# A two-block transformer kernel: the softmax of block 2's first layer normalised on GpSimd ahead of the transposes

## What is computed

```python
q = apply_rope(rms_norm(heads(aq, N_Q_HEADS), q_norm), cos, sin)
k = apply_rope(rms_norm(heads(ak, N_KV_HEADS), k_norm), cos, sin)
y_a = global_gqa(q, k, v, k_c, v_c)        # 256 sequence rows attend to sequence and context
y_ca = context_attention(q_c, k_c, v_c)    # 256 context rows attend to the context only
```

## Time and profile before

| | |
|---|---|
| median of 3 runs | 1485.29 us (1481.9 to 1487.43) |
| profiled execution, its own time | 1483.27 us |
| its span, first to last instruction | 1481.5 us |
| TensorE matmul busy | 1419.3 us, 96% of the span |
| TensorE weight load busy | 1150.1 us, 78% |
| one low part of the weights on VectorE (L1902), mean of 344 | 1.213 us |
| VectorE, ScalarE, GpSimd busy | 917.6, 773.5, 152.7 us |
| mean granted clock of TensorE | 0.987 of full |

### The profile page before, as it was taken

One profiled execution on the slowest core, in us unless ns is written; L12 is line 12 of the kernel. 1 busy time (PEld: TensorE's weight loads), 2 busy tenths in 40 slices (PEclk: granted clock), 3 DMA queues, 4 the chain that ended last, 5 costly groups with the idle time before them and its releaser, 6 DMA issues.

```text
span 1481.5 us, 21298 instructions
## 1 busy us (share of the span) xinstructions
PE 1419.3 (96%) x8232; PEld 1150.1 (78%) x8232; DVE 917.6 (62%) x1618; ACT 773.5 (52%) x1281; POOL 152.7 (10%) x188
## 2 busy tenths in 40 slices
PE   7999989999999999998999999999999789999998
PEld 6887767799887787776789978787777348777776
DVE  4555668666544554566856666577553775669665
ACT  5445776455444444687445545334456322544873
POOL 6040000000000000000000000002000660132220
PEclk9999999999999999999999999999999899999999
DMA  9784326697555755332689654463223001255100
GB/s 280 253 189 121 121 90 246 180 272 212 185 185 171 281 174 169 96 130 89 238 243 250 194 181 164 167 170 86 58 80 92 25 1 57 73 164 142 58 30 29
DMA packets 183555, 220.29 MB, mean 149 GB/s; under 512 B 6667, under 2 KB 103477, under 8 KB 183456
## 3 DMA queue, kind: packets, MB, share of 16 engines
q1 hardware_dynamic: 179376, 211.65, 45.4%
q0 software_dynamic: 3040, 7.28, 2.6%
q10 hardware_dynamic: 1040, 0.00, 0.0%
HBM read 215.90 MB, written 3.01 MB: 148 GB/s over the span
## 4 chain that ended last, share of the span: by engine, by line
PE 41%; DVE 8%; ACT 3%; issue 2%; POOL 1%; DVEq 0%; ACTq 0%
PE bank L634 10%; PE bank L636 10%; PE bank L635 10%; PE bank L1150 2%; PE bank L1113 1%; DVE w_low L1902 1%; PE bank L1126 1%; PE bank L651 1%; DVE arena L2322 1%; PE bank L1289 1%; ACT w_high L1430 1%; PE bank L721 1%; DVE arena L2419 1%; PE bank L1309 0%; PE bank L1297 0%
## 5 line engine op out<-in xcount | busy, mean ns | idle before, releaser
L1902 DVE TENSOR_TENSOR w_low<-raw,w_high 128x1024 fp32r<-128x1024 f32 x344 | 413.4, 1213 | 296.1 <-ACT w_high L1430 292.0
L1430 ACT ACTIVATE w_high<-raw 128x1024 fp32r<-128x1024 f32 x352 | 364.8, 1046 | 327.2 <-PE bank L636 257.9
L634 PE MATMUL bank<-w_high,acts_r 128*128 128x512 f32 (+1 forms) x848 | 342.5, 404 | 19.3 <-DVE arena L2153 10.7
L636 PE MATMUL bank<-w_high,acts_r 128*128 128x512 f32 (+1 forms) x848 | 332.7, 392 | 0.0
L635 PE MATMUL bank<-w_low,acts_r 128*128 128x512 f32 (+1 forms) x848 | 332.5, 392 | 0.0
L634 PE MATMUL bank<-acts_r,w_high 128*128 128x256 f32 (+1 forms) x736 | 229.8, 312 | 1.3 <-DVE arena L2381 1.3
L636 PE MATMUL bank<-acts_r,w_low 128*128 128x256 f32 (+1 forms) x736 | 226.5, 308 | 0.0
L635 PE MATMUL bank<-acts_r,w_high 128*128 128x256 f32 (+1 forms) x736 | 225.4, 306 | 0.0
L634 PEld LDWEIGHTS bank<-w_high,acts_r 128*128 128x128 f32 x848 | 161.0, 190 | 67.1 <-DVE arena L2153 13.3
L636 PEld LDWEIGHTS bank<-w_high,acts_r 128*128 128x128 f32 x848 | 161.3, 190 | 37.2
L635 PEld LDWEIGHTS bank<-w_low,acts_r 128*128 128x128 f32 x848 | 161.6, 191 | 32.9 <-issue 0.2
(11 more groups left out here) (331 smaller groups left out, 1713.1 us busy)
## 6 DMA issues: line engine op xcount, KB each, us to landing
raw<-in_w_in SPq DMA_DIRECT2D x69, 1024.0 KB, 5.1
raw<-in_w_up SPq DMA_DIRECT2D x64, 512.0 KB, 6.9
raw<-in_w_down SPq DMA_DIRECT2D x32, 1024.0 KB, 4.9
raw<-in_w_ada SPq DMA_DIRECT2D x24, 1024.0 KB, 7.7
raw<-in_w_in SPq DMA_DIRECT2D x34, 512.0 KB, 5.1
raw<-in_w_o SPq DMA_DIRECT2D x8, 1024.0 KB, 8.0
raw<-in_w_out SPq DMA_DIRECT2D x8, 1024.0 KB, 5.0
raw<-in_w_out_c SPq DMA_DIRECT2D x4, 768.0 KB, 4.9
```

The lines of the kernel that those rows point to most:

```text
L634: mm(o, lh, rh, start=start, stop=False)
L636: return mm(o, ll, rh, start=False, stop=stop)
L1430: run(A_(high, src, ACT.Copy), (high_ready, n + 1))
L1902: run(V.tensor_tensor(low, src, high.bitcast(F32), ALU.subtract), split_done(n))
```

## The change

In layer 0 of block 2 GpSimd multiplies each unit's exponentials, in place, by the inverse of their sum, as soon as VectorE has inverted it; the transposes wait for that (`probs_scaled`). The product that spreads the inverse sums, ScalarE's copy of it and VectorE's product with it are dropped; VectorE copies the PSUM result instead. GpSimd's other work of this stretch is put between the pairs: the four folds behind pair 5, the five DMAs behind pair 12.

```diff
@@ second
-                    pe.wait_ge(*probs_at(2 + l, u))
+                    pe.wait_ge(*(probs_at(3, u) if l else (probs_scaled, u + 1)))
@@ values
-                    pe.wait_ge(*pair_inverted.at(2 + l, i))
+                    if l:
+                        pe.wait_ge(*pair_inverted.at(3, i))
...
-                    for side in range(2):
+                    for side in range(2 if l else 0):
                         inverse = stat[:, (u + side) % 4, 3, 1:2].to_broadcast([P, DH])
                         ins = mm(o[side * DH:(side + 1) * DH, P:2 * P], inverse, ident[:, :], start=True, stop=True)
@@ attention2 of ScalarE
-                    if i >= 2:
+                    if l and i >= 2:
                         spread_sums(i - 2)
...
-                spread_sums(PAIRS - 1)
+                if l:
+                    spread_sums(PAIRS - 1)
@@ take_values
-                    dve.wait_ge(*sum_spread.at(2 + l, i))
-                    run(V.tensor_tensor(dst, o[:, 0:P], spread[:, :], ALU.mult), emptied("o", 2 + l, i))
+                    if l == 0:
+                        dve.wait_ge(*filled("o", 2, i))
+                        run(V.tensor_copy(dst, o[:, 0:P]), emptied("o", 2, i))
+                        return
+                    dve.wait_ge(*sum_spread.at(3, i))
+                    run(V.tensor_tensor(dst, o[:, 0:P], spread[:, :], ALU.mult), emptied("o", 3, i))
@@ GpSimd's list
-            for c in range(4):
-                pool.wait_ge(*emptied("in2f", 0, c))
-                z = uc[:, c, :].rearrange("p (s n) -> p s n", s=2)
...
-            pool.wait_ge(*filled("s", 2, 22))
-            pool.wait_ge(*filled("s", 2, 23))
-            pool.dma_start(decay.rearrange("p t n -> p (t n)"), C["decay"]).then_inc(decay_loaded, 16)
...
+            for i in range(PAIRS):
+                pool.wait_ge(*pair_inverted.at(2, i))
+                for u in (2 * i, 2 * i + 1):
+                    row = S4[:, u % 4, 0:SEQ if units_of_block2(0)[u][2] >= TILES else N4]
+                    G.tensor_scalar(row, row, stat[:, u % 4, 3, 1:2], None, ALU.mult).then_inc(probs_scaled, 1)
+                if i == 5:
+                    for c in range(4):
+                        pool.wait_ge(*emptied("in2f", 0, c))
+                        z = uc[:, c, :].rearrange("p (s n) -> p s n", s=2)
...
+                if i == 12:
+                    pool.wait_ge(*filled("s", 2, 22))
+                    pool.wait_ge(*filled("s", 2, 23))
+                    pool.dma_start(decay.rearrange("p t n -> p (t n)"), C["decay"]).then_inc(decay_loaded, 16)
...
```

More of the change, by code:

```diff
@@ L461, in two_blocks @@
         pair_inverted = Signal(sem("pair_inverted"), soft_pairs + [(l, i) for l in (2, 3) for i in range(len(units_of_block2(l - 2)) // 2)])
-        sum_spread = Signal(sem("sum_spread"), soft_pairs + [(l, i) for l in (2, 3) for i in range(len(units_of_block2(l - 2)) // 2)])
+        sum_spread = Signal(sem("sum_spread"), soft_pairs + [(3, i) for i in range(len(units_of_block2(1)) // 2)])
+        probs_scaled = sem("probs_scaled")
         stick_summed = Signal(sem("stick_summed"), sticks)
@@ L1149, in values @@
                                 v = nv[:, b, h * DH:(h + 1) * DH]
-                            mm(o[side * DH:(side + 1) * DH, 0:P], v, PT2[:, side, n * P:(n + 1) * P], start=n == 0, stop=n == len(blocks) - 1)
-                    for side in range(2):
+                            ins = mm(o[side * DH:(side + 1) * DH, 0:P], v, PT2[:, side, n * P:(n + 1) * P],
+                                     start=n == 0, stop=n == len(blocks) - 1)
+                    for side in range(2 if l else 0):
                         inverse = stat[:, (u + side) % 4, 3, 1:2].to_broadcast([P, DH])
@@ L2728, in _ @@
                 pool.dma_start(dst, src).then_inc(hidden_loaded, 16)
-            for c in range(4):
-                pool.wait_ge(*emptied("in2f", 0, c))
-                z = uc[:, c, :].rearrange("p (s n) -> p s n", s=2)
[L2732 to L2737, removed]
-            pool.wait_ge(*filled("s", 2, 22))
-            pool.wait_ge(*filled("s", 2, 23))
-            pool.dma_start(decay.rearrange("p t n -> p (t n)"), C["decay"]).then_inc(decay_loaded, 16)
-            for n in range(4):
-                pool.dma_start(w3[n], A["hy_w3_2"][0][:, n * HY:(n + 1) * HY]).then_inc(w3_loaded, 16)
+            for i in range(PAIRS):
[7 more added lines that the diff above has]
+                        z = uc[:, c, :].rearrange("p (s n) -> p s n", s=2)
+                        left, right, right_back = z[:, :, 0:P], z[:, :, P:SEQ], z[:, :, SEQ - 1:P - 1:-1]
+                        run(G.tensor_tensor(left, left, right_back, ALU.subtract))
+                        run.settle()
+                        run(G.tensor_tensor(right, right, right, ALU.add))
+                        run.settle()
+                        run(G.tensor_tensor(right_back, right_back, left, ALU.add), (z_folded, c + 1))
+                if i == 12:
+                    pool.wait_ge(*filled("s", 2, 22))
+                    pool.wait_ge(*filled("s", 2, 23))
+                    pool.dma_start(decay.rearrange("p t n -> p (t n)"), C["decay"]).then_inc(decay_loaded, 16)
+                    for n in range(4):
+                        pool.dma_start(w3[n], A["hy_w3_2"][0][:, n * HY:(n + 1) * HY]).then_inc(w3_loaded, 16)
             for i in range(PAIRS):
```

## The result

| | before | changed |
|---|---|---|
| median of 4 runs each | 1483.6 us (1481.8 to 1487.4) | 1499.0 us (1496.9 to 1501.0) |
| ratio to before, 95% interval | | 1.0095 (1.0077 to 1.0114) |
| profiled execution | 1483.27 us | 1496.92 us |
| its span | 1481.5 us | 1495.1 us |

The change makes the kernel 0.95% slower, 15.4 us in the medians. The profiled execution of the changed kernel is the fastest of its four, so the profiles explain 13.65 us and not the 1.8 us more of the medians. The forecast was 1491, 0.4%, with a range from 1484 to 1500. Every line number of the attention has moved by a few in the changed file: scores are L1114, transposes L1127, values L1152, the reciprocal L2446, the multiply L2741, low parts L1906.

A forecast was written before the change was run, and what follows sets the result against it. TensorE's own list was taken to set the attention's pace: -4.2 us gained, +8.6 waits and +1.7 clock make +6.1 us, which against the median of 1485.3 gave 1491 us, range 1484 to 1500.

The forecast's parts named there:

- rival 3: GpSimd's multiplies are slow, growing with columns: at 1.6 us waits of 18 us, +17, 1502 us in all; chance 0.10.
- What a multiply costs: GpSimd's multiply by a scalar from SBUF: taken as 1.0 us for 512 columns and 0.7 for 256.
- rival 1: GpSimd's multiplies are short, 0.6 to 0.8 us; only pairs 0 and 6 wait notably; +1.6, 1487 us; chance 0.20.
- Wide after narrow: Transposes of pairs 4 and 8: 9.69 us from scores against TensorE's 8.95, wait 0.75 us each, 1.5.
- Wide after wide: Transposes of pairs 5 and 9: a loop of 8.85 us against TensorE's 8.14, wait 0.7 us each, 1.4.
- Pairs 12 and 13: Wide pairs with one product where the convolution's four stood: 8.6 us, under 8.95, so no wait.
- Pair 1: Like pair 9, but with four more late-head transposes (0.44 us) in its round: wait 0.3 us.
- Narrow pairs: Transposes of narrow pairs fit without a wait: 7.83 us against TensorE's 7.92.
- Pair 0: First pair's transposes wait 2.1 us for the multiplies, its reciprocal counted 0.4 us earlier because the folds leave this place.
- Pair 6: Its multiplies queue on GpSimd behind pair 5's multiplies and four folds; TensorE waits 3.3 us, the costliest pair.
- The gain: Dropped inverse-sum products free TensorE 0.28 us a pair (0.24 to 0.32), 15 counted: -4.2 us.
- The clock: A low-clock stretch after TensorE's waits in pairs 0 and 6: one drop counted (none to two), +1.7 us.

The follow-up runs named there:

- experiment 2: Changed kernel with its four folds spread, one each behind pairs 2, 3, 6 and 7, not all behind pair 5: 1492.7 us, ratio to before 1.0062.
- experiment 3: Changed kernel with VectorE's reciprocal of pair 0 alone moved ahead of its round's low parts and convolution products: 1495.8 us, ratio to before 1.008.
- Experiment 1: Changed kernel without GpSimd's multiplies and without the wait for them, output left undivided: 1479.4 us, ratio to before 0.9974.
- experiment 5: Changed kernel with GpSimd multiplying only the first half of each row, 256 of 512 columns or 128 of 256: 1489.8 us, ratio to before 1.0034.
- experiment 6: Changed kernel with the multiplies on VectorE right behind the reciprocal, GpSimd keeping folds and DMAs: 1482.1 us, ratio to before 0.9986.
- experiment 4: Changed kernel with every reciprocal of this layer ahead of its round's low part and features, folds spread behind pairs 2, 3, 6, 7: 1481.1 us.
- experiment 7: Changed kernel with every reciprocal of this layer ahead of its round's low part and features, folds still behind pair 5: 1481.9 us.
- experiment 8: Changed kernel with the multiplies on VectorE and every reciprocal ahead of the low part: 1481.4 us, ratio to before 0.9979.

## Why the forecast came out as it did

The direction, the place and the mechanism of the waits were right; the size was short, by 7.6 us in the profiled executions (13.65 against 6.1). Of these, 5.9 are waits, 0.9 the gain and 0.7 the clock. That the median still lies within the range, 1 us from its end, is partly luck. The range was laid on a median before of 1485.3, which came out as 1483.6. The measured 15.4 us on top of that would be 1500.7. The sum's own bounds ended at +12 us, and rival 3, whose multiplies these were, was left out of the range with a chance of 0.10. By the forecast's steps:

- **What a multiply costs** is the step that failed. It was taken as 1.0 and 0.7 us, from one multiply of 128 columns and the price of a column in a memset, and is 1.56 and 0.92: a column costs 2.5 ns, twice the memset's 1.21. The row of 0.542 us for 128 columns was a good guide (0.603 here); the slope laid on it was not. The bound named for two tensors, 1.276 us for 512 columns, was no bound: one tensor and a scalar from SBUF take longer. Rival 3, with 1.6 us, described this run: it gave 18 us of waits, and the table has 14.5 without the clock. The page of the Trainium skill named in rival 1 (GPSIMD Engine Reference, Performance versus the Vector engine) gives 769 ns for 512 elements as its best case. This instruction took 1562 ns here, twice that.
- **Wide after narrow** (pairs 4, 8): the forecast's own sum with the measured length is 7.49 + 0.2 + 3.1 - 8.95 = 1.8; measured 1.75 and 1.70. **Wide after wide** (5, 9): 6.65 + 3.3 - 8.14 = 1.8; measured 1.65. Pairs 12 and 13, which were to fit, would wait 0.8 by the same sum and waited 0.66 and 0.56. The chains were read rightly, only one term in them was short, and it counts twice in each pair. Pair 1, forecast at 0.3, waited nothing in the changed kernel, because the half clock ahead of it had slowed TensorE; in experiments 2 and 3, without that, it waited 1.2.
- **Narrow pairs** nearly fit. With the measured length the loop is 6.23 + 0.2 + 1.8 = 8.2 against 7.92; with the folds out of its way, in experiment 2, pair 6's round is 7.50 against 7.34 without waits, and pair 7's 7.75 against 7.66. The others show none.
- **Pair 0** waited 3.1 in place of 2.1; its reciprocal did come 0.4 us earlier, as forecast, since the folds had left the place (3.49 us for the three low parts, 4.02 before).
- **Pair 6** waited 3.43, forecast 3.3: the length of a multiply enters here with 0.4 us, the folds with 9.6.
- **The gain** is 3.3 us, forecast 4.2: 0.22 a pair, below the lower bound of 0.24. Experiment 1 shows it alone. The lower bound took 0.06 us a record from the values' matmuls; what the last four records cost less than that is not shown.
- **The clock** cost 2.4 us in the profile, forecast 1.7 for one drop. Experiments 2, 3, 5 and 6 show it at pair 0, at pair 6, or at neither.
- The five DMAs cost nothing that shows: pair 13's multiplies came behind 3.0 us of idle time of GpSimd, and did not queue behind them.
- The last question of the forecast, whether the stage behind the attention would move by itself, is answered by the starts: 13.72 us later at the last values, 13.6 at the end of the span. Each profile has a half-clock stretch behind the attention at a place where the other has none (from 1325 us on before, from 1383 on in the changed kernel), and they happen to cost the same.

What the forecast did not ask is where the reciprocal could go. It named VectorE's low part and convolution as links of the loop, and took their order as given. Experiments 4, 7 and 8 show that with another order the waits go, but for the folds and for 0.4 to 1.0 us in pair 0's round: the reciprocal needs nothing of low part and convolution, and VectorE stands idle when its sums are ready (1.20 us ahead of the one in experiment 4's rows). Either cure alone ends the waits of the wide pairs behind pair 0: an earlier reciprocal, or a multiply of a third of the length (experiment 6).

## What to carry to other kernels

Work given to an idle engine lies on the path for the stretch between its input and its consumer, not in the engine's free time: measure that stretch, pair by pair, and then see what stands ahead of the producer in its own queue, because moving that producer forward may be free. Time a multiply on GpSimd at its real length and with its real operands before it is put between two engines; here a short multiply and a memset together gave half the slope. And what stands in an in-order queue between two such links holds the second one up by all of its length that the slack does not cover: the folds, 9.6 us of them, held pair 6 up by 3.4.

## What the runs showed of the hardware

- GpSimd's product of a 128-partition fp32 tile with a scalar for each partition from SBUF takes 603, 921 and 1562 ns for 128, 256 and 512 columns (changed kernel and experiment 5); a product or sum of two tiles of 512 takes 1276. VectorE does the one of 512 in 484 ns (experiment 8) and took 0.82 us each for the two of pair 0 that met GpSimd's folds (experiment 6).
- In experiment 4 a multiply whose turn came while a low part (two operands in SBUF) ran on VectorE took 1.73 us, with 256 columns as with 512. A multiply already under way when the low part began kept its 0.92 or 1.57 us, and the low part its 1.23.
- Between GpSimd's folds (two operands in SBUF too) and VectorE both sides were stretched: at 1076.66 in the changed kernel a fold took 1.59 us in place of 0.73 and the low part beside it 1.43 in place of 1.22.
- One idle time of TensorE of 1.65 us was followed by 3.4 us at half the clock in experiment 6; waits of 2.68 and 0.46 us were not in the changed kernel's profile, and waits of 2.71 and 0.46 were in experiment 3's.
